# Decoder step, one core: the first two units of seven stages side by side, sums in front of the last tile, cache loads one by one, key stores last, eight banks for the first embedding

## Chip, core and metric

The kernel runs as one program on one core of a Trainium2 chip. The time is the device time of one execution in microseconds (us); it was 1290.23 as the median of three executions before the change. Beside them one execution was profiled, and all times of single instructions come from that one.

## What is computed

One inference step of a two-layer decoder trunk for 256 prompt positions and 8 sample rows together, so 264 columns. The first layer has a Mamba-2 mixer, the second an attention over a shared key/value pair; both have a half feed-forward block before and after the mixer and a gated embedding at the end:

```python
def trunk(x, p, ...):
    for i in range(DEPTH):                       # 2 layers
        x = x + 0.5 * swiglu(rmsnorm(x, w['ffn1_norm'][i]), w['ffn1_wi'][i], w['ffn1_wo'][i])
        h = rmsnorm(x, w['mix_norm'][i])
        if i < N_A_LAYERS:
            out, ... = mamba2_mixer(h, ...)
        else:
            q = rope(rmsnorm((h @ w['w_q'][j]).reshape(...), w['q_norm'][j]), pos)
            out = window_attention(q, k_all, v_all, hist_valid, w['attn_sinks'][j]) @ w['w_o'][j]
        x = x + out
        x = x + 0.5 * swiglu(rmsnorm(x, w['ffn2_norm'][i]), w['ffn2_wi'][i], w['ffn2_wo'][i])
        gate = jax.nn.sigmoid(rmsnorm(x, w['ple_norm'][i]) @ w['ple_gate'][i])
        x = x + gate * (p[i] @ w['ple_proj'][i])
        if i == N_A_LAYERS - 1:
            k_new, v_new = shared_kv(x, w['kv_norm'], w['w_kv'], w['k_norm'], pos)
```

Here `swiglu` is `(silu(gate) * up) @ wo`, and `rmsnorm` divides each row by the root of its mean square. All data are float32.

## The kernel before, in words

**Units and stages.** The weights are a list of 369 units of 128 x 1024 numbers (512 KB each), used in order by 17 stages. In the order of the program: f1i0 (first feed-forward block, inner product, 44 units), f1o0 (outer, 22), sin (mixer's input, 49), sout (16), f2i0 (44), pp0 (first embedding, 2), f2o0 (22), pg0 (gate, 8), f1i1 (44), kv (4), f1o1 (22), q (8), pp1 (2), o (8), f2i1 (44), f2o1 (22), pg1 (8). A ring of four slots takes them: SyncE loads a unit into `raw` as soon as the slot's last low half is done, ScalarE rounds it to `whi` (`round_unit`, L943), VectorE subtracts to get the low half `wlo` (`low_unit`, L1334). Both are called through `ahead(stage, i, j)`, which converts the unit four places further on than unit j of the stage, once TensorE is done with that slot.

**Products.** A product of a 128x128 weight tile and a 128x264 activation tile is three matmuls (`split_products`, L428 to L430: high by high, high by low, low by high). A unit of an inner stage ("A": f1i, sin, pg, kv, q) has 8 tiles along the depth, so 24 matmuls into one bank. A unit of an outer stage adds into all eight banks.

**A handoff.** At the end of an outer stage VectorE adds each of the eight banks to `x` (L1364), ScalarE rounds the tile to `xh` (L978) and squares it (L981), VectorE makes `xl` (L1353), and GpSimd adds the squares up (L1933, `add_squares`; in f2i0 TensorE does this with 16 passes). The next stage's first unit waits tile by tile for `xl` (`x_wait`); after its second unit TensorE sums the squares over the rows (`sums`, L460), ScalarE takes the root (`root`, L999), VectorE the reciprocal (`row_factor`, L1375), and only then can VectorE take a finished unit out of its bank (`take`, L1381). The last two units of the stage before are converted early, so that units 0 and 1 of a new stage are ready at the handoff; units 2 and 3 are converted right after the split of `x`, and units 4 and 5 (`ahead(stage, 0, 0)` and `(0, 1)`) before the root. A function of ScalarE whose table isn't loaded puts an ACT_TABLE_LOAD ahead of it.

**What orders the rest.** Each engine runs its own list in the order in which the code stands; semaphores tie them together. In f1i1 the stage kv's activations (8 `xh`, 8 `xl`) are made after the first four units. In kv, VectorE takes four units of keys and values (`kf`, `vf`), between them `ahead("kv", 0, j)`; ScalarE then takes two roots (L1223, L1224) for the key norm. GpSimd updates the state of the sample rows beside stages f2i0 to f1i1 with loads and stores of 1 MB, then issues the two cache loads `kc` and `vc` (L2082, L2083), and in q, behind the rotated keys, four stores of keys and values (L2092 to L2095), the cosine products of the queries (`query_cos`, L2102) and the small inverse roots. Loads from SyncE run in queue q1, those of GpSimd in q0. In q TensorE alternates query units, rotations (`turn`), scores (L531 to L535), transposes (L546) and weighted sums for eight pairs of heads.

```python
def first_units(stage, n, b_wait, **ops):
    for j in range(n):
        unit_a(stage, 0, j, b_wait if j < 4 else None, x_wait=(j == 0), **ops)
        if j == 1:
            sums(stage, b_wait)
```

## Time and profile before

| | |
|---|---|
| median of 3 executions | 1290.23 us (1288.71 to 1290.67) |
| the profiled execution | 1291.22 us, span 1289.4 us |
| TensorE matmuls | busy 1228.4 us, 95% |
| VectorE / ScalarE / GpSimd | 887.5 us (69%) / 690.4 us (54%) / 234.8 us (18%) |
| granted TensorE clock, mean | 0.98 |
| chain that ended last | TensorE 69%, VectorE 15%, ScalarE 7%, issue 7% |
| read from memory, mean rate | 226.87 MB, 186 GB/s |

TensorE's busy time counts matmuls that overlap, so 95% doesn't mean that 5% is all there is to gain: a matmul of 264 columns is shown with 0.28 us, while the next begins 0.12 us after it. To see what a stretch costs, one looks at the starts.

### The profile page before, as it was taken

The numbers are of one execution on the slowest core, as the hardware profiler recorded it, in microseconds if no ns is written. First come the engines' busy times: TensorE is split into PE (matmuls) and PEld (weight loads), VectorE is DVE, ScalarE is ACT, GpSimd is POOL, SyncE is SP. The second block draws the span as 40 slices with busy tenths as digits, with TensorE's granted clock in tenths as the row PEclk, the third lists the DMA queues.
The fourth block names the chain that finished last, engine by engine and source line by source line (L and its number), as shares of the span: only waits on it lengthen the run. The fifth ranks groups of instructions, "written<-read, shape, count | busy, mean of one in ns | idle before, by whom it ended". The sixth has DMA issues, their size and how long they took to land.

```text
span 1289.4 us, 26817 instructions
## 1 busy us (share of the span) xinstructions
PE 1228.4 (95%) x9921; PEld 1187.0 (92%) x9921; DVE 887.5 (69%) x1412; ACT 690.4 (54%) x1100; POOL 234.8 (18%) x333
## 2 busy tenths in 40 slices
PE   5999999789999999999999899998998999999998
PEld 5999999778898899999999799998987899999998
DVE  5677646788888876677646878786466758667447
ACT  5444436576566555555546664554364546454335
POOL 3000003112231100122344223332015201000001
PEclk8999999899999999999999899998998999999999
DMA  8555555534344445767776656756541135455552
GB/s 311 190 179 184 180 179 174 202 110 177 135 149 143 153 147 190 310 211 254 261 289 204 225 195 230 255 199 241 179 170 64 50 120 175 179 179 179 179 179 83
DMA packets 61280, 239.08 MB, mean 185 GB/s; under 512 B 7064, under 2 KB 8256, under 8 KB 56704
## 3 DMA queue, kind: packets, MB, share of 16 engines
q1 hardware_dynamic: 54864, 197.01, 43.5%
q0 software_dynamic: 6064, 40.66, 8.8%
q8 instruction: 42, 0.69, 0.2%
q10 hardware_dynamic: 288, 0.54, 0.1%
q14 instruction: 22, 0.18, 0.0%
HBM read 226.87 MB, written 13.39 MB: 186 GB/s over the span
## 4 chain that ended last, share of the span: by engine, by line
PE 69%; DVE 15%; ACT 7%; issue 7%; DMA 1%; POOL 1%; DVEq 0%; SPq 0%; ACTq 0%; POOLq 0%
PE bank L428 21%; PE bank L429 21%; PE bank L430 21%; DVE wlo L1334 3%; ACT whi L943 3%; DVE xl L1353 2%; DVE gu L1393 1%; DVE xact L1575 1%; DVE x L1364 1%; DVE gu L1381 1%; PE bank L546 1%; POOL sq L1933 1%; DMA raw<-weights 1%; PE bank L740 1%; PE bank L735 1%
## 5 line engine op out<-in xcount | busy, mean ns | idle before, releaser
L1334 DVE TENSOR_TENSOR wlo<-raw,whi 128x1024 fp32r<-128x1024 f32 x369 | 459.4, 1248 | 278.5 <-ACT whi L943 277.5
L428 PE MATMUL bank<-xh,whi 128*128 128x264 f32 x2024 | 589.1, 291 | 21.3 <-DVE xl L1353 18.4
L429 PE MATMUL bank<-xl,whi 128*128 128x264 f32 x2024 | 578.6, 286 | 0.0
L430 PE MATMUL bank<-xh,wlo 128*128 128x264 f32 x2024 | 577.9, 286 | 0.0
L943 ACT ACTIVATE whi<-raw 128x1024 fp32r<-128x1024 f32 x369 | 387.6, 1054 | 291.0 <-PE bank L430 277.5
L428 PEld LDWEIGHTS bank<-xh,whi 128*128 128x128 f32 x2024 | 386.8, 191 | 32.6 <-DVE xl L1353 15.9
L429 PEld LDWEIGHTS bank<-xl,whi 128*128 128x128 f32 x2024 | 387.0, 191 | 0.9
L430 PEld LDWEIGHTS bank<-xh,wlo 128*128 128x128 f32 x2024 | 384.7, 190 | 0.0
L428 PE MATMUL bank<-hh,whi 128*128 (+1 forms) x896 | 257.0, 287 | 5.2 <-DVE xact L1381 3.4
L430 PE MATMUL bank<-hh,wlo 128*128 (+1 forms) x896 | 256.1, 286 | 0.0
L429 PE MATMUL bank<-hl,whi 128*128 (+1 forms) x896 | 255.5, 285 | 0.0
L428 PEld LDWEIGHTS bank<-hh,whi 128*128 128x128 f32 x896 | 169.7, 189 | 7.0 <-DVE xact L1381 3.6
L429 PEld LDWEIGHTS bank<-hl,whi 128*128 128x128 f32 x896 | 170.2, 190 | 0.1
L430 PEld LDWEIGHTS bank<-hh,wlo 128*128 128x128 f32 x896 | 169.7, 189 | 0.0
L1933 POOL TENSOR_TENSOR sq<-sq 128x264 f32<-128x264 f32 x49 | 44.0, 897 | 507.6 <-ACT sq L981 502.3
L1009 ACT ACTIVATE hh<-gu 128x264 fp32r<-128x264 f32 (+1 forms) x88 | 37.3, 424 | 161.8 <-DVE gu L1393 161.8
L1381 DVE TENSOR_TENSOR gu<-bank,rstd 128x264 f32<-128x264 f32 x192 | 82.2, 430 | 19.8 <-PE bank L430 17.6
L1398 DVE TENSOR_TENSOR hl<-gu,hh 128x264 f32 (+1 forms) x88 | 42.4, 482 | 28.9 <-ACT hh L1009 28.9
L2056 POOL TENSOR_TENSOR xact<-xact,da_bc 128x512 f32<-128x512 f32 x32 | 39.5, 1235 | 106.7 <-PE bank L430 106.6
L1575 DVE SCALAR_TENSOR_TENSOR xact<-under,vs,xact 128x256 f32<-128x256 f32 x96 | 46.6, 486 | 2.3
L1393 DVE TENSOR_TENSOR gu<-gu 128x264 f32<-128x264 f32 x88 | 44.9, 511 | 0.6 <-ACT gu L1004 0.6
L1353 DVE SCALAR_TENSOR_TENSOR xl<-x,vs,xh 128x264 fp32r<-128x264 f32 x64 | 38.7, 616 | 3.1 <-ACT xh L978 3.0
(309 smaller groups left out, 1005.6 us busy)
## 6 DMA issues: line engine op xcount, KB each, us to landing
raw<-weights SPq DMA_DIRECT2D x369, 512.0 KB, 3.5
under<-ssm POOLq DMA_DIRECT2D x8, 1024.0 KB, 5.8
xact<-ssm POOLq DMA_DIRECT2D x8, 1024.0 KB, 7.0
out_ssm_s<-xact POOLq DMA_DIRECT2D x8, 1024.0 KB, 5.4
xact<-dtx_rows POOLq DMA_DIRECT2D x5, 1024.0 KB, 9.5
zs<-dtx_rows POOLq DMA_DIRECT2D x2, 1024.0 KB, 13.5
x<-xT SPq DMA_DIRECT2D x1, 1056.0 KB, 5.6
xact<-stat_rows POOLq DMA_DIRECT2D x2, 528.0 KB, 6.9
```

The source lines that it names most:

```text
L428: pe.matmul(out, whi[:, w, c], rh, start=start, stop=False)
L429: pe.matmul(out, whi[:, w, c], rl, start=False, stop=False)
L430: return pe.matmul(out, wlo[:, w, c], rh, start=False, stop=stop)
L943: act.activation(whi[:, s, :], raw[:, s, :], ACT.Copy).then_inc(hi_ready, 1)
L1334: dve.tensor_tensor(wlo[:, s, :], raw[:, s, :], whi[:, s, :].bitcast(F32), ALU.subtract).then_inc(lo_ready, 1)
L1353: dve.scalar_tensor_tensor(out=xl[:, m, :], in0=x[:, m, :], scalar=vs[:, gain + m:gain + m + 1], in1=xh[:, m, :].bitcast(F32), op0=ALU.mul ...
L1381: dve.tensor_tensor(dst, src[:, 0:N], rstd[:, :], ALU.mult).then_inc(a_free, 1)
L1393: dve.tensor_tensor(gu[:, 2 * p + 1, :], gu[:, 2 * p, :], gu[:, 2 * p + 1, :], ALU.mult).then_inc(h_ready, 1)
L1398: dve.tensor_tensor(one(hl), gu[:, 2 * p + 1, :], one(hh).bitcast(F32), ALU.subtract).then_inc(hl_ready, 1)
L1575: dve.scalar_tensor_tensor(out=out, in0=xr[:, k:k + T], scalar=vs[:, V_CW + CT * k + c:V_CW + CT * k + c + 1], in1=out, op0=ALU.mult, op1= ...
L1933: pool.tensor_tensor(sq3[:, 0, :], sq3[:, 0, :], sq3[:, m, :], ALU.add).then_inc(sq_pair, 1)
L2056: pool.tensor_tensor(by_head(part), by_head(part), da_bc[:, 2 * k:2 * k + 2, 4 * q:4 * q + 4].unsqueeze(3).to_broadcast([P, 2, 4, 64]), AL ...
```

## The change

- Seven stages (sin, f2i0, pg0, f1i1, q, f2i1, pg1) run their first two units side by side, tile by tile into two banks (`unit_pair`); `sums` stand in front of the last tile (in f1i1 behind unit 2). f1i0 is as it was.
- The table of the square root is loaded at the head of `split_x` and, in the first `gates`, at the eighth tile. The root and the reciprocal come before the conversion of units 4 and 5, which now stands behind the first takes (in sin, behind the first take).
- In q the third query unit is cut in two halves around the two rotations; the constants, the embedding's `ph` and `pl` and two conversions are moved behind the first rotations.
- GpSimd issues the second cache load once the first has landed and the keys are multiplied by the cosine. The key and value stores stand behind the last small inverse root. The memset of `minus_half` is moved to the front.
- The first embedding (pp0) writes its eight tiles into eight banks, where it used four in turn; f2o0 waits for the copies of the four upper ones.

Cut to its core (lines are shifted to the left):

```diff
+FIRST_EMBED_BANK = [4, 5, 6, 7] + [(A0["pp0"] + _m) % 4 for _m in range(4)]
...
-def first_units(stage, n, b_wait, **ops):
-    for j in range(n):
-        unit_a(stage, 0, j, b_wait if j < 4 else None, x_wait=(j == 0), **ops)
-        if j == 1:
+def unit_pair(stage, b_wait, sums_inside=True, rh=xh, rl=xl):
+    u = U0[stage]
+    banks_ = [(A0[stage] + j) % 4 for j in range(2)] if stage not in ("sin", "q") else [0, 1]
+    for j in range(2):
+        pe.wait_ge(a_free, A0[stage] + j + 1)
+        if b_wait is not None:
+            pe.wait_ge(b_free, 8 * b_wait + banks_[j] + 1)
+    pe.wait_ge(lo_ready, u + 2)
+    for k in range(KT):
+        if sums_inside and k == KT - 1:
             sums(stage, b_wait)
+        pe.wait_ge(xl_ready, XREADY[stage] + k + 1)
+        for j in range(2):
+            mm = split_products(bank[banks_[j]][:, 0:N], (u + j) % RING, k, rh[:, k, :], rl[:, k, :], k == 0, k == KT - 1)
+    mm.then_inc(unit_used, 2)
+def first_units(stage, b_wait, rh=xh, rl=xl):
+    if stage == "f1i0":
+        for j in range(4):
+            unit_a(stage, 0, j, x_wait=(j == 0))
+            if j == 1:
+                sums(stage)
+        return
+    unit_pair(stage, b_wait, stage != "f1i1", rh, rl)
+    for j in (2, 3):
+        unit_a(stage, 0, j, b_wait, rh=rh, rl=rl)
+        if j == 2 and stage == "f1i1":
+            sums(stage)
 def first_units_p(stage, b_wait):
-    for j in range(KT):
-        unit_a(stage, 0, j, x_wait=(j == 0))
-        if j == 1:
-            sums(stage, b_wait)
-def query_unit(t):
+    unit_pair(stage, b_wait)
+    for j in range(2, KT):
+        unit_a(stage, 0, j)
+def query_unit(t, tiles=range(KT)):
...
     else:
         pe.wait_ge(a_free, A0["q"] + t + 3)
-    for k in range(KT):
-        if t == 0:
-            pe.wait_ge(xl_ready, XREADY["q"] + k + 1)
+    for k in tiles:
         mm = split_products(bank[QUERY_BANK[t]][:, 0:N], u % RING, k, xh[:, k, :], xl[:, k, :], k == 0, k == KT - 1)
-    mm.then_inc(unit_used, 1)
+    if KT - 1 in tiles:
+        mm.then_inc(unit_used, 1)
...
 def ffn_in(stage, b_wait, aside=None, **ops):
-    first_units(stage, 4, b_wait, **ops)
+    first_units(stage, b_wait, **ops)
...
     for m in order:
+        if first and stage == "f2o0" and m >= 4:
+            pe.wait_ge(a_free, A0["pp0"] + m - 4 + 1 + 4)
...
         for m in range(4):
-            a = A0[stage] + 4 * j + m
-            pe.wait_ge(a_free, a + 1)
+            if j == 0:
+                if m == 1:
+                    pe.wait_ge(dtx_row, 1)
+                pe.wait_ge(a_free, A0[stage] + 1)
+            else:
+                pe.wait_ge(a_free, A0[stage] + m + 1)
             for k in range(2):
-                mm = split_products(bank[a % 4][:, 0:N], s, 2 * m + k, ph[:, k, :], pl[:, k, :], k == 0, k == 1)
+                mm = split_products(bank[FIRST_EMBED_BANK[4 * j + m]][:, 0:N], s, 2 * m + k, ph[:, k, :], pl[:, k, :], k == 0, k == 1)
...
     else:
...
     for k in range(KT):
-        if j == 0:
-            pe.wait_ge(xl_ready, XREADY["sin"] + k + 1)
...
     mm.then_inc(unit_used, 1)
-    if j == 1:
-        sums("sin", 0)
...
 for s_ in range(len(SIN)):
-    sin_unit(s_)
+    if s_ == 1:
+        unit_pair("sin", 0)
+    elif s_ > 1:
+        sin_unit(s_)
...
-query_unit(0)
-query_unit(1)
-sums("q", 3)
+unit_pair("q", 3)
 key_turn()
-query_unit(2)
+query_unit(2, range(4))
...
 turn(1)
+query_unit(2, range(4, KT))
...
 def split_x(gain, b_stage, stage=None, n=0):
+    act.preload_act_table(ACT.Sqrt)
...
-    ahead(stage, 0, 0)
-    ahead(stage, 0, 1)
-    if stage in NORM:
+    if stage == "f1i0":
+        ahead(stage, 0, 0)
+        ahead(stage, 0, 1)
         root(stage)
-    act.preload_act_table(ACT.Silu)
+        act.preload_act_table(ACT.Silu)
+    else:
+        root(stage)
+        act.preload_act_table(ACT.Silu)
+        ahead(stage, 0, 0)
+        ahead(stage, 0, 1)
...
 def gates(gate, layer, gain):
     root(gate)
+    act.preload_act_table(ACT.Sigmoid)
...
             act.activation(gu[:, j % 4, :], gu[:, j % 4, :], ACT.Sigmoid).then_inc(sig_done, 1)
+        if j == KT - 1 and gain is not None:
+            act.preload_act_table(ACT.Sqrt)
...
+root("sin")
 ahead("sin", 0, 0)
-root("sin")
...
-act.activation(ident_r, ident, ACT.Copy)
-act.activation(mask_all, mask, ACT.Copy).then_inc(mask_ready, 1)
-split_p(1)
...
-ahead("q", 0, 0)
-act.preload_act_table(ACT.Sqrt)
-ahead("q", 0, 1)
...
 query_square(0)
+query_square(1)
...
 act.activation(vtok, bank[5][:, :].rearrange("p (c n) -> p c n", c=2), ACT.Copy).then_inc(v_tok, 1)
-query_square(1)
+act.activation(ident_r, ident, ACT.Copy)
+act.activation(mask_all, mask, ACT.Copy).then_inc(mask_ready, 1)
+ahead("q", 0, 0)
 query_square(2)
+ahead("q", 0, 1)
+split_p(1)
...
-    ahead(stage, 0, 0)
-    ahead(stage, 0, 1)
-    if stage in NORM:
-        row_factor(stage)
+    if stage == "f1i0":
+        ahead(stage, 0, 0)
+        ahead(stage, 0, 1)
+    row_factor(stage)
...
     up(0, 0)
+    if stage != "f1i0":
+        ahead(stage, 0, 0)
+        ahead(stage, 0, 1)
...
             else:
                 dve.wait_ge(unit_used, U0[stage] + j + 1 + RING)
-            dve.tensor_copy(pj[layer][4 * j + m], bank[(A0[stage] + 4 * j + m) % 4][:, 0:N]).then_inc(a_free, 1)
+            dve.tensor_copy(pj[layer][4 * j + m], bank[FIRST_EMBED_BANK[4 * j + m]][:, 0:N]).then_inc(a_free, 1)
...
     if kind == "dt":
-        ahead("sin", 0, 0)
...
         dt_take()
+        ahead("sin", 0, 0)
...
                   vs[:, V_SINK:V_SINK + AH].rearrange("p (t b) -> p t b", t=PAIRS).unsqueeze(2).to_broadcast([P, PAIRS, 2, 2]), -1.0, None, ALU.mult)
-low_p(1)
-ahead("q", 0, 0)
-ahead("q", 0, 1)
...
 key_rope()
-take(qf[:, 2, :], "q", 2)
 for t in range(2):
...
     rope_add(t)
+take(qf[:, 2, :], "q", 2)
+ahead("q", 0, 0)
+ahead("q", 0, 1)
+low_p(1)
...
 pool.dma_start(kc, kcT).then_inc(cache_in, 16)
-pool.dma_start(vc, vc_in).then_inc(cache_in, 16)
+link(pool, pool_step, steps, pool.memset(minus_half, -0.5))
...
 for j in range(2):
...
     pool.tensor_tensor(gu[:, j, :], kf[:, j, :], cosT, ALU.mult).then_inc(k_cos, 1)
+pool.wait_ge(cache_in, 16)
+pool.dma_start(vc, vc_in).then_inc(cache_in, 16)
 add_squares("q")
-pool.wait_ge(k_roped, 2)
-pool.wait_ge(v_tok, 1)
-pool.dma_start(kv_p[0], kf[:, :, 128:256]).then_inc(kv_out, 16)
-pool.dma_start(kv_p[1], vf[:, :, 128:256]).then_inc(kv_out, 16)
-pool.dma_start(kv_new[0], kf[:, :, T:N]).then_inc(kv_out, 16)
-pool.dma_start(kv_new[1], vf[:, :, T:N]).then_inc(kv_out, 16)
...
-link(pool, pool_step, steps, pool.memset(minus_half, -0.5))
+pool.wait_ge(q_gains, 1)
+pool.wait_ge(k_roped, 1)
 query_cos(0)
-pool.wait_ge(q_gains, 1)
+pool.wait_ge(k_roped, 2)
...
 inverse_root(row_r, row_m, row_u, 1, dec_r)
+pool.dma_start(kv_p[0], kf[:, :, 128:256]).then_inc(kv_out, 16)
+pool.dma_start(kv_p[1], vf[:, :, 128:256]).then_inc(kv_out, 16)
+pool.dma_start(kv_new[0], kf[:, :, T:N]).then_inc(kv_out, 16)
+pool.dma_start(kv_new[1], vf[:, :, T:N]).then_inc(kv_out, 16)
```

Three places show how the order of instructions changes. TensorE at the handoff to f2i1, before, from the last tile of unit 1 (bank 2) on; `sq,cs` is the sum of squares:

```order
L428 MATMUL bank2<-xh,whi 128x264
L429 MATMUL bank2<-xl,whi 128x264
L430 MATMUL bank2<-xh,wlo 128x264
L460 MATMUL bank45<-sq,cs 128x264
L428 MATMUL bank3<-xh,whi 128x264
L429 MATMUL bank3<-xl,whi 128x264
L430 MATMUL bank3<-xh,wlo 128x264
```

and after:

```order
L433 MATMUL bank2<-xl,whi 128x264
L434 MATMUL bank2<-xh,wlo 128x264
L464 MATMUL bank45<-sq,cs 128x264
L432 MATMUL bank1<-xh,whi 128x264
L433 MATMUL bank1<-xl,whi 128x264
L434 MATMUL bank1<-xh,wlo 128x264
L432 MATMUL bank2<-xh,whi 128x264
L433 MATMUL bank2<-xl,whi 128x264
L434 MATMUL bank2<-xh,wlo 128x264
L432 MATMUL bank3<-xh,whi 128x264
L433 MATMUL bank3<-xl,whi 128x264
L434 MATMUL bank3<-xh,wlo 128x264
```

The last two tiles of both units (banks 1 and 2) now alternate, and the sum stands one tile before their end, with unit 2 (bank 3) behind.

ScalarE at the same handoff, before, from the last tile of the split on, where the four `whi` are units 2 to 5:

```order
L978 ACTIVATE xh<-x,vs 128x264
L981 ACTIVATE sq<-x 128x264
L943 ACTIVATE whi<-raw 128x1024 x4
L999 ACT_TABLE_LOAD
L999 ACTIVATE rstd<-bank,cs 128x264
L1015 ACT_TABLE_LOAD
L1004 ACTIVATE gu<-gu 128x264
L943 ACTIVATE whi<-raw 128x1024
```

and after:

```order
L1009 ACTIVATE xh<-x,vs 128x264
L1012 ACTIVATE sq<-x 128x264
L974 ACTIVATE whi<-raw 128x1024 x2
L1031 ACTIVATE rstd<-bank,cs 128x264
L1050 ACT_TABLE_LOAD
L974 ACTIVATE whi<-raw 128x1024 x2
L1036 ACTIVATE gu<-gu 128x264
L974 ACTIVATE whi<-raw 128x1024
```

One table load is gone from the front of the root (it stands before the first `xh`), and two of the four conversions stand behind the root.

GpSimd behind the last state store, up to the first cosine of the queries, before:

```order
L2082 DMA xact<-kcT 128x2048
L2083 DMA xact<-vcT 128x2048
L2084 TENSOR_SCALAR xact<-cs,vs 128x264
L2085 TENSOR_SCALAR xact<-cs,vs 128x128
L2088 TENSOR_TENSOR gu<-xact,cs 128x264 x2
L1933 TENSOR_TENSOR sq<-sq 128x264 x7
L2092 DMA out_kv_p<-xact 256x1x128
L2093 DMA out_kv_p<-xact 256x1x128
L2094 DMA out_kv_new<-xact 256x1x8
L2095 DMA out_kv_new<-xact 256x1x8
L2112 MEMSET small 128x4
L2102 TENSOR_TENSOR gu<-xact 128x264 x2
```

and after:

```order
L2123 DMA xact<-kcT 128x2048
L2124 MEMSET small 128x4
L2125 TENSOR_SCALAR xact<-cs,vs 128x264
L2126 TENSOR_SCALAR xact<-cs,vs 128x128
L2129 TENSOR_TENSOR gu<-xact,cs 128x264 x2
L2131 DMA xact<-vcT 128x2048
L1974 TENSOR_TENSOR sq<-sq 128x264 x7
L2138 TENSOR_TENSOR gu<-xact 128x264 x2
```

The load of `vcT` has moved behind the two key products, and the four stores no longer stand ahead of the cosines.

## Rows read from the trace of the kernel before

**Rows 1.** Waits of TensorE: engine, line, releaser: us in total, times, longest.

```profile
PE bank L428 <- DVE xl L1353: 18.4, 19, 8.5
```

**Rows 2.** Timeline at the handoff to f2i1: start, us, engine, line, operation, [idle before].

```profile
1062.13 0.52 ACT L978 ACTIVATE xh<-x,vs 128x264 fp32r<-128x264 f32 x1 [1.64 <-DVE x L1364]
...
1064.67 5.27 POOL L1933 TENSOR_TENSOR sq<-sq 128x264 f32<-128x264 f32 x6
...
1067.81 1.53 DVE L1353 SCALAR_TENSOR_TENSOR xl<-x,vs,xh 128x264 fp32r<-128x264 f32 x2
...
1069.73 3.57 DVE L1334 TENSOR_TENSOR wlo<-raw,whi 128x1024 fp32r<-128x1024 f32 x3 [0.39 <-ACT whi L943]
...
1072.78 0.61 PE L460 MATMUL bank<-sq,cs 128*128 128x264 f32 x2
...
1074.11 1.28 ACT L999 ACT_TABLE_LOAD   x1
...
1075.92 1.80 DVE L1375 RECIPROCAL rstd<-rstd 128x264 f32<-128x264 f32 x1 [0.57 <-ACT rstd L999]
```

**Rows 3.** Timeline of the stage sin.

```profile
219.88 1.80 DVE L1375 RECIPROCAL rstd<-rstd 128x264 f32<-128x264 f32 x1 [0.61 <-ACT rstd L999]
...
240.61 0.36 PE L809 MATMUL bank<-cs,small 64*128 64x64 f32 x1 [6.77 <-ACT small L1154]
```

**Rows 4.** Timeline at the handoff to f2i0.

```profile
504.44 3.72 PE L460 MATMUL bank<-sq,cs 128*128 128x264 f32 x16
```

**Rows 5.** Timeline of the first embedding.

```profile
634.93 0.36 PE L428 MATMUL bank<-ph,whi 128*128 128x264 f32 x1 [1.90 <-DVE xact L1446]
```

**Rows 6.** Timeline of pg0 and f1i1; one stretch: us, busy, PEclk, DMA share, GB/s.

```profile
715.93 1.07 ACT L943 ACTIVATE whi<-raw 128x1024 fp32r<-128x1024 f32 x1 [0.42 <-DMA raw<-weights]
...
718.05 1.22 DVE L1334 TENSOR_TENSOR wlo<-raw,whi 128x1024 fp32r<-128x1024 f32 x1
...
736.47 1.29 DVE L1353 SCALAR_TENSOR_TENSOR xl<-x,vs,xh 128x264 fp32r<-128x264 f32 x3
...
738.00:742.00 4.00, 4.00 (x20) 4.00 (x19) 1.23 (x1) 1.06 (x1) 0.37 (x1) 0.50 0.01 4
...
743.90 0.61 PE L460 MATMUL bank<-sq,cs 128*128 128x264 f32 x2
...
762.16 0.38 PE L428 MATMUL bank<-xh,whi 128*128 128x264 f32 x1 [0.25 <-DVE wlo L1334]
```

**Rows 7.** Timeline from kv to f1o1; DMA queues from 879 to 880 us.

```profile
872.48 0.54 POOL L2082 DMA_DIRECT2D xact<-kcT  x1 [6.07 <-DMA out_ssm_s<-xact]
...
882.96 1.06 ACT L943 ACTIVATE whi<-raw 128x1024 fp32r<-128x1024 f32 x1 [4.37 <-DMA raw<-weights]
...
885.86 1.06 ACT L943 ACTIVATE whi<-raw 128x1024 fp32r<-128x1024 f32 x1 [1.85 <-DMA raw<-weights]
...
889.14 0.59 PE L428 MATMUL bank<-hh,whi 128*128 128x264 f32 x1 [1.18 <-ACT gu L1224]
...
q0 software_dynamic: 33, 0.27, 65.6%
q1 hardware_dynamic: 33, 0.14, 32.8%
```

**Rows 8.** Timeline of the stage q.

```profile
951.97 6.20 POOL L1933 TENSOR_TENSOR sq<-sq 128x264 f32<-128x264 f32 x7 [56.16 <-ACT sq L981]
...
968.90 0.74 POOL L2092 DMA_DIRECT2D out_kv_p<-xact  x1 [10.72 <-DVE xact L1492]
...
973.80 1.01 PE L531 MATMUL bank<-hl 128*128 128x384 f32 x2 [2.23 <-DVE xact L1508]
...
982.59 1.60 PE L546 MATMUL bank<-under 128*128 128x128 f32 x12
```

**Rows 9.** Timeline of the last two units of pg1.

```profile
1282.27 0.43 DVE L1381 TENSOR_TENSOR gu<-bank,rstd 128x264 f32<-128x264 f32 x1 [1.43 <-PE bank L430]
...
1285.17 0.43 DVE L1381 TENSOR_TENSOR gu<-bank,rstd 128x264 f32<-128x264 f32 x1 [1.66 <-PE bank L430]
```

## Prediction

> **What bounds the kernel now.** I read three views in this order: what TensorE waits for, the timeline around every handoff from one stage to the next, and the DMA queues where a weight unit comes late. Inside the stages TensorE is the bound: at the end of the program VectorE takes finished units at 1282.27 and 1285.17 and had to wait for TensorE before each [rows 9]. That is 2.90 us for a unit, and with 24 matmuls in a unit 0.121 us for one matmul. Time is therefore only to be had where TensorE waits or runs slow, and nearly all of that sits at handoffs: its longest total is for the low half `xl` of the new activations, 19 waits and 18.4 us, of which 8.5 are the start of the program [rows 1]. At the others the first unit of a stage is fed one tile of `xl` at a time while the second unit, whose weights are ready, stands behind it.
>
> **The sum, place by place.** The stage f2i1 is the pattern. `xl` tiles 6 and 7 take 1.53 us for both and the last is ready at 1069.34; GpSimd has added the squares at 1069.94; the sums start at 1072.78, after two whole units [rows 2]. Side by side, six matmuls (0.73 us) go with each tile, less than the 0.77 us in which a tile comes, so that after the last tile only the sums and six matmuls are left. The sums stand in front of the last tile and wait for GpSimd, so they start at about 1070.0, the pair is through 0.73 us plus the sums later, and unit 2 starts 1072.78 - (1070.0 + 0.73) = 2.05 us earlier. Its low half is the first of three from 1069.73, ready at 1070.95, so it doesn't wait. Is the gain kept? The row factor now comes before the low halves of units 4 and 5: two conversions end at 1072.15, the reciprocal (1.80) then runs to 1074.0 where it ended at 1077.72 [rows 2], two takes bring 1074.8 and the low half of unit 4 is ready near 1076.0. TensorE wants it at 1070.98 + 2 x 2.90 = 1076.8. It is kept with 0.8 us to spare: **f2i1 2.05 us**. The last stage, pg1, has the same tiles, and its end hangs on TensorE alone [rows 9]; its sums wait for GpSimd equally, so **pg1 2.0 us**.
>
> The square root's table load leaves the path there: it stood at 1074.11 for 1.28 us [rows 2] between the sums and the root, and now runs at the head of the split, where ScalarE waits 1.64 us for the first sum `x` [rows 2]. It costs nothing as long as that wait is over 1.28 us. There the row goes against a rule. The Trainium skill (ScalarE: Activation LUTs, What ACT_TABLE_LOAD costs) gives 2.66 us for a switch, a drain of 1.38 us counted in. By that price each of the six loads moved into a split would hold the first tile 1.02 us and the total gain would be 6 us smaller; the trace shows no such drain, so I leave it out.
>
> Stage sin: the first two conversions of this stage would end 1.1 us before the third, so the reciprocal that began at 219.88 [rows 3] can begin at about 218.15, 1.73 us earlier. Behind it comes a chain of small steps on VectorE and ScalarE that ends in TensorE's wait of 6.77 us up to 240.61 [rows 3]. TensorE's own gain of some 2 us there only lengthens that wait; what counts is the chain's shift. The conversion moved behind the first take lies in VectorE's wait for the exponential. **sin 1.7 us**, from 0 (if the three state loads, now issued some 3 us earlier, hold a weight unit) to 2.
>
> Stage f2i0 adds its squares on TensorE: 16 passes, 3.3 of the 3.72 us [rows 4], and these stay. Only the gaps between tiles go: **0.8 us** (0.5 to 1.1).
>
> The first embedding waits 1.90 us at 634.93 for a bank that VectorE has yet to copy [rows 5]. With eight banks the wait goes, but the next stage wants four of them back, and the same copies are then late. Between 0 and 1.9: **1.0 us**.
>
> Stages pg0 and f1i1 belong together, since in pg0 VectorE's chain of take, gate, add, conversion and `xl` decides. The row factor is 1.8 us earlier, as in sin, but the chain meets a weight unit that landed at 715.93 [rows 6] behind two GpSimd loads, which don't move: ScalarE's half of the conversion ends at 717.0 and VectorE's begins at 718.05 [rows 6], so 1.05 us of the 1.8 are left. The last `xl` of f1i1 is ready at 737.76 now [rows 6], 736.7 then. TensorE runs at the granted clock 0.50 there, its 1.2 GHz level, with 20 matmuls in 4 us, and the sums come at 743.90 [rows 6]. With the pair, 6 matmuls are left after the last tile where 27 were. If the clock stays low until about 741.5, the sums, which stand behind unit 2 here, come near 743.5, hardly earlier than now; the root is then 1.3 us earlier by its table load and 1.2 by the conversion it no longer waits for. But now two conversions (2.44 us) stand behind it, before unit 8, whose low half TensorE waited for at 762.16 [rows 6] after VectorE's eight `xl` of the key stage. By my count it is ready at about 760.5: **1.6 us** for both stages, from 0 to 4.8 (if the clock stays at its 2.4 GHz level throughout).
>
> The largest place is the key stage and the start of f1o1. A cache load of 1 MB is issued at 872.48 and a second right behind it, and weight units issued right behind land so late that ScalarE can convert them only from 882.96 (4.37 us of waiting) and from 885.86 [rows 7]. The key values' last take and their square roots stand behind these two conversions on VectorE and ScalarE; TensorE waits for them until 889.14 [rows 7]. While both run, queue 0 moves 0.27 MB/us and queue 1, the weights', 0.14, with 33 packets each [rows 7]. With one cache load instead of two, 1 MB at 0.27 MB/us from about 874.5 ends near 878.5; the weights then have the whole rate, and their two units land at about 879 and 881. Then conversion, table load (1.28), two roots (about 1.0) give 884.3 in place of 889.1: 4.8 us. And the 18 matmuls that ran behind that wait on the low clock need 0.1 us less each if it isn't there for the clock to fall in: 1.8 us, of which I take 1.5. **6.3 us**, from 2.9 (weights land at 881 and 883) to 7.4. The second cache load goes out behind the key norms, beside f1o1, where a unit has some 8 us to land. The Trainium skill (DMA: Bandwidth & Descriptors, Queues, rings and completion order) says that each DMA engine takes packets of its queues in turn; the equal packets of the row agree. By it one cache load still takes two thirds of the bytes while it lasts, which is the low end above.
>
> In the stage q the four key stores are issued from 968.90 on, GpSimd's first two `q` cosines come behind them, and TensorE's first scores wait for what follows until 973.80 [rows 8]. The stores go behind the last query. The new order, worked out from durations: sums at 958.2, when GpSimd's squares end (951.97 + 6.20 [rows 8]), root 958.9, reciprocal (behind two conversions) 960.6 to 962.4, takes 963.2, key rotation 964.8, first cosine 964.4 to 965.2, second rotation 966.2, half a unit of filler to 967.7, scores at 967.7. Then VectorE has a take, two conversions and the low half of `p` (4.1 us) before the first maxima, at 971.5; exponentials 975.2, first transposes 976.6 in place of 982.59 [rows 8]. From there on the rhythm is TensorE's and doesn't change: **q 6.0 us**, from 4.5 (GpSimd slower beside VectorE) to 7.
>
> Sum: 2.05 + 2.0 + 1.7 + 0.8 + 1.0 + 1.6 + 6.3 + 6.0 = 21.45 us. The profiled execution took 1291.22 us for a span of 1289.4; it is 1.0 over the median 1290.23. 1291.22 - 21.45 = 1269.8, and against the median **1268.8 us**.
>
> **Rivals.** (A) One cache load holds the weights as long as two did, because the share and not the volume decides: the key stage gives 0, and the time is 1275.1. For it: the first unit behind the loads could only be converted 10.5 us after them. Against it: the 1 MB store just before, for which the loads waited 6.07 us [rows 7], held no conversion up. (B) The clock of f1i1 stays up, since twice the work comes with each tile: 3.2 us more, 1265.6. Against it: even then three quarters of the time is waiting. (C) VectorE gives back what TensorE gains, because conversions moved behind the row factor end later than TensorE wants them: sin, pg0 and f1i1 at 0, f2i1 at 1.0; 1273.1. The margin of 0.8 us in f2i1 decides. (D) The other side: pairs are fed thinly enough that TensorE's clock falls at all seven handoffs. A spell as in f1i1 (20 matmuls in 4 us where 33 would go) costs 3.9 us over its 8 us, seven are 27.3: 1268.8 + 27.3 = 1296.1, slower. It decides if TensorE waits as long between a pair's tiles as it does in f1i1; at six of seven places the rows leave 0.6 us at most for a tile.
>
> **How the numbers follow.** Forecast 0.60, A 0.12, B 0.10, C 0.12, D 0.03, anything else 0.03. The range from 1263 to 1277.5 takes in A, B and C and leaves out D and joint mishaps. A measurement tells about 0.2% (2.6 us) from no change: faster by more 0.95, within 0.02, slower 0.03.
>
> **What would show it.** In the profile after: sums of f2i1 within 0.2 us of GpSimd's last square; no table load between sums and root; conversions of the two weight units at 879 to 881 instead of 883 to 886, and a granted clock of 1.0 through f1o1's first unit; first scores about 6 us nearer to the last `xl` of q; the wait before `small` in sin as long as now. The forecast is wrong if weight units still land after 9 us beside one cache load, or if VectorE's conversion of unit 4 becomes what TensorE waits for in the feed-forward stages.

## The result and the profile after

The median of five executions is 1277.60 us (1276.56 to 1282.18), against 1290.23 before: the ratio is 0.9917 (0.9895 to 0.9939). In a second group of runs the same kernel took 1275.25 us beside 1289.52 (ratio 0.9876, 0.9859 to 0.9893). So by the medians the kernel is 12.6 to 14.3 us faster where 21.4 were forecast, and the median lies 0.1 us outside the range. The times are scattered more widely than before: three of the eleven executions took 1281.5 to 1282.5 us, the other eight 1272.8 to 1277.8. The profiled one took 1281.47 for a span of 1279.4, so it is one of the three.

To see where the gain is, I cut both profiled executions at points that each has: the first sum `x<-bank,x` of each handoff and the sums of the key squares.

| stretch | before, us | after, us | gain | forecast |
|---|---|---|---|---|
| start, to the first sum in front of sin | 207.61 | 208.16 | -0.55 | 0 |
| sin and sout | 286.76 | 283.97 | 2.79 | 1.7 |
| f2i0, pp0, f2o0 | 204.64 | 202.75 | 1.89 | 0.8 + 1.0 |
| pg0, f1i1, kv up to the key sums | 181.44 | 181.82 | -0.38 | 1.6 |
| from there over f1o1 to q | 69.43 | 68.35 | 1.08 | 6.3 |
| q, pp1, o | 111.79 | 110.37 | 1.42 | 6.0 |
| f2i1, f2o1 | 194.32 | 192.43 | 1.89 | 2.05 |
| pg1 | 33.40 | 31.60 | 1.80 | 2.0 |

Four terms came about as forecast. One was too small (sin), and three failed: pg0 with f1i1, the key stage, q. In the waits of TensorE (engine, line, releaser: us in total, times, longest) the answer to [rows 1] is that 18.4 us over 19 waits for `xl` have become 11.7 over 4. The waits for `wlo`, the low halves, have grown from 0.9 us over 3 to 7.1 over 6. A wait for the exponentials is new:

```profile
PE bank L432 <- DVE xl L1391: 11.7, 4, 8.5
PE bank L432 <- DVE wlo L1372: 7.1, 6, 2.5
...
PE bank L558 <- ACT small L1295: 2.4, 1, 2.4
```

The handoff to f2i1, the answer to [rows 2] (timeline: start, us, engine, line, operation, [idle before]):

```profile
1057.52 6.22 POOL L1974 TENSOR_TENSOR sq<-sq 128x264 f32<-128x264 f32 x7 [35.60 <-ACT sq L1012]
...
1061.57 1.55 DVE L1391 SCALAR_TENSOR_TENSOR xl<-x,vs,xh 128x264 fp32r<-128x264 f32 x2
...
1063.87 0.63 PE L464 MATMUL bank<-sq,cs 128*128 128x264 f32 x2
...
1065.04 1.28 ACT L1050 ACT_TABLE_LOAD   x1
...
1065.88 1.79 DVE L1413 RECIPROCAL rstd<-rstd 128x264 f32<-128x264 f32 x1
```

GpSimd's squares (`sq<-sq`) end at 1063.74 and the sums start 0.13 us later, as forecast. No table load stands between sums and root; the one that is left runs behind the root. The reciprocal starts 2.0 us behind the sums, where it was 3.1.

pg0 and f1i1, the answer to [rows 6]:

```profile
713.38 1.06 ACT L974 ACTIVATE whi<-raw 128x1024 fp32r<-128x1024 f32 x1 [3.87 <-DMA raw<-weights]
...
724.63 0.56 PE L432 MATMUL bank<-xh,whi 128*128 128x264 f32 x1 [2.52 <-DVE wlo L1372]
...
733.46 0.96 POOL L1974 TENSOR_TENSOR sq<-sq 128x264 f32<-128x264 f32 x1 [0.34 <-ACT sq L1012]
...
740.19 0.61 PE L464 MATMUL bank<-sq,cs 128*128 128x264 f32 x2
...
746.03 0.39 PE L432 MATMUL bank<-xh,whi 128*128 128x264 f32 x1 [2.34 <-DVE wlo L1372]
```

ScalarE waits 3.87 us for the weight unit for which it waited 0.42 before. The last `xl` of f1i1 is ready at 734.71: the program was 4.1 us ahead of before at the start of pg0, and here it is 3.05 ahead. The longest wait for a low half (2.52 us) stands at the head of the pair in f1i1, which starts only when the low halves of both its units are there; behind it TensorE waits for `xl` twice more. The sums come 5.8 us after the last square (at 734.42), because unit 2 stands ahead of them, and TensorE is at the 1.2 GHz level for the first part of that time (granted clock 0.57 from 734 to 738 us, 1.00 from 738 to 741). Then it waits 2.34 us for the low half of unit 4, which was moved behind the row factor. From the last `xl` to the key sums the program gains 0.7 us.

The key stage, the answer to [rows 7]; the last row is a stretch of four us (from, to, length, busy times and counts of PE, PEld, DVE, ACT, POOL, then the granted clock, DMA share, GB/s):

```profile
868.61 0.54 POOL L2123 DMA_DIRECT2D xact<-kcT  x1 [5.95 <-DMA out_ssm_s<-xact]
...
879.49 2.09 ACT L974 ACTIVATE whi<-raw 128x1024 fp32r<-128x1024 f32 x2 [4.66 <-DMA raw<-weights]
...
882.20 0.59 PE L432 MATMUL bank<-hh,whi 128*128 128x264 f32 x1 [3.73 <-DVE xact L1419]
...
884.00:888.00 4.00, 4.00 (x21) 4.00 (x21) 3.96 (x3) 1.06 (x1) 0.15 (x1) 0.52 0.58 189
```

The whole program is 3.76 us ahead of before at the key sums. The first conversion is 3.47 us ahead and so a little late by comparison; the second follows at once and has gained 1.5 us. The wait of TensorE (3.73 us) is still there, and so is the spell at the 1.2 GHz level behind it (granted clock 0.52 in the last row). The two weight units behind the cache load took 10.1 and 9.3 us to land.

In q, the answer to [rows 8], the first scores come 17.80 us after the first sum of the stage, where it was 23.92:

```profile
962.85 0.51 PE L558 MATMUL bank<-hl 128*128 128x384 f32 x2
...
970.62 0.98 PE L558 MATMUL bank<-hl 128*128 128x384 f32 x2 [2.42 <-ACT small L1295]
...
973.12 2.29 PE L573 MATMUL bank<-under 128*128 128x128 f32 x9
...
980.91 0.61 PE L558 MATMUL bank<-hl 128*128 128x384 f32 x2
```

That is 6.1 us, the forecast. Yet the third scores (980.91) come only 3.0 us earlier than before by the same count: 10.3 us pass between second and third, where before it was 7.6. The first transposes (973.12) are 4.6 us earlier, where the sum had 6.0. The second scores take 0.98 us for their first two matmuls, the third 0.61.

### The profile page after: what moved, and what is told of

It is laid out like the page before. It is cut to its first block, busy times and chain, and to the rows that moved or that the text cites. A ratio compares the mean times of both kernels' runs of the same rounds, so it can differ in the third digit from the quotient of the medians.

```text
span 1279.4 us, 26823 instructions
## 1 busy us (share of the span) xinstructions
PE 1224.1 (96%) x9921; PEld 1187.4 (93%) x9921; DVE 885.9 (69%) x1412; ACT 691.6 (54%) x1101; POOL 234.0 (18%) x333
## 4 chain that ended last, share of the span: by engine, by line
PE 71%; DVE 14%; issue 6%; ACT 6%; DMA 2%; POOL 1%; DVEq 0%; SPq 0%; ACTq 0%; POOLq 0%
PE bank L432 21%; PE bank L433 21%; PE bank L434 21%; DVE wlo L1372 4%; ACT whi L974 2%; DMA raw<-weights 1%; DVE xact L1616 1%; DVE gu L1431 1%; DVE xl L1391 1%; DVE gu L1419 1%; PE bank L573 1%; POOL sq L1974 1%; DVE x L1402 1%; PE bank L773 1%; PE bank L768 1%
## 5 line engine op out<-in xcount | busy, mean ns | idle before, releaser
L432 PE MATMUL bank<-xh,whi 128*128 128x264 f32 x2024 | 586.4, 290 | 20.4 <-DVE xl L1391 11.7
## 6 DMA issues: line engine op xcount, KB each, us to landing
xact<-dtx_rows POOLq DMA_DIRECT2D x5, 1024.0 KB, 10.6
```

What stands on the lines that cost most here:

```text
L432: pe.matmul(out, whi[:, w, c], rh, start=start, stop=False)
```

## The experiments

The first four kernels are the changed one with one edit or none. The others are built on the second of them, with both cache loads late, so that again one place at a time differs. The table has what the profiled executions gave; the column "low" is the time at the 1.2 GHz level in two stretches of q to o (12 to 38 and 60 to 90 us after the first sum), worked out as twice the part by which the mean granted clock of a stretch is under 1, times its length. The column "median" has all executions of a kernel, the others the profiled one alone. In three columns the same code repeats within 0.1 us (f2i1 with f2o1, pg1, and f2i0 to f2o0, which isn't shown), but not in all: pg0 to the key sums took 180.5 to 182.2 us in the eight profiles whose code is the same there.

| kernel | pg0, f1i1 | key, f1o1 | q, pp1, o | low | f2i1, f2o1 | pg1 | median |
|---|---|---|---|---|---|---|---|
| before | 181.4 | 69.4 | 111.8 | 14.0 | 194.3 | 33.4 | 1290.23 |
| after | 181.8 | 68.3 | 110.4 | 13.4 | 192.4 | 31.6 | 1277.60 |
| after, again | 182.2 | 67.9 | 110.5 | 13.4 | 192.4 | 31.6 | 1275.25 |
| both cache loads late | 181.9 | 62.4 | 111.9 | 16.8 | 192.4 | 31.6 | 1276.39 |
| cache loads together | 180.5 | 67.4 | 109.2 | 9.8 | 192.4 | 31.6 | 1279.36 |
| key stores early | 182.2 | 63.9 | 111.5 | 16.6 | 192.4 | 31.6 | 1277.37 |
| maxima first | 181.6 | 62.8 | 106.9 | 10.4 | 192.4 | 31.6 | 1272.03 |
| f1i1, unit 4 first | 182.1 | 62.4 | 111.9 | 16.8 | 192.4 | 31.6 | 1274.59 |
| pg0, load later | 180.8 | 62.4 | 105.9 | 3.6 | 192.4 | 31.6 | 1270.12 |
| no pairs at the end | 181.8 | 62.3 | 107.3 | 7.0 | 194.3 | 33.4 | 1279.82 |
| f1i1, sums inside | 178.1 | 62.3 | 108.8 | 10.2 | 192.4 | 31.6 | 1271.00 |
| four edits together | 176.6 | 62.4 | 104.5 | 3.6 | 192.4 | 31.6 | 1264.48 |
| filler matmuls | 182.1 | 62.4 | 108.9 | 10.0 | 192.4 | 31.6 | 1272.34 |

**The changed kernel again**

> The changed kernel as it is, beside the others of this group, as their measure. Its profiled execution (1281.47 us) stood some 4 us over three of its other four. Theory one: the 4 us come from one place, where a transfer of GpSimd meets the weight loads (stage pg0 or the key stage); then one of the two execution times shows weight units landing later there, and the two groups of times appear again, near 1277 and 1282. Theory two: they come from chance in the granted clock; then the spells at the 1.2 GHz level differ in number between the executions and the landings don't. The time expected is 1276.5 to 1282.

Six executions: 1272.81, 1273.10, 1274.90, 1275.60, 1277.80 and, the profiled one, 1282.49. Its profile agrees with the first one (110.5 for 110.4 in q, 67.9 for 68.3 in the key stage). The two groups of times appeared again. Both profiles lie in the upper group, so they show what the kernel does in three executions of eleven, and the others gain more. No profile shows where, so neither theory is decided; the next runs show two places where the same code takes different times, the key stage and q.

**Both cache loads behind the key norms**

```diff
-            pool.dma_start(kc, kcT).then_inc(cache_in, 16)
...
                 pool.tensor_tensor(gu[:, j, :], kf[:, j, :], cosT, ALU.mult).then_inc(k_cos, 1)
+            pool.dma_start(kc, kcT).then_inc(cache_in, 16)
             pool.wait_ge(cache_in, 16)
             pool.dma_start(vc, vc_in).then_inc(cache_in, 16)
```

> The first cache load too is issued behind the key norms, the second still when the first has landed; no cache load lies beside the key stage any more. Theory V (the one load left beside the weights is what still holds them): the two conversions of weight units that ended their wait at 879.5 and 880.5 in the changed kernel come at about 875 and 876.5, TensorE's wait of 4.0 us and the clock spell behind it go, and the kernel is 4 to 6 us faster than the changed one. Theory S (the weights are late there for another reason, the store of the last state or SyncE's queue): the two conversions stay within 1 us of where they are, and the time is the same within 1 us. If the load meets another stage's weights instead, f1o1 shows it as a DMA wait of ScalarE behind 890 us.

The conversions and what follows, and the load at its new place:

```profile
876.35 1.06 ACT L974 ACTIVATE whi<-raw 128x1024 fp32r<-128x1024 f32 x1 [1.18 <-PE bank L434]
...
879.61 3.45 DVE L1521 RECIPROCAL gu<-gu 128x528 f32<-128x528 f32 x1 [0.94 <-ACT gu L1264]
...
886.25 0.60 POOL L2129 DMA_DIRECT2D xact<-kcT  x1
```

ScalarE no longer waits for a transfer but for TensorE, the reciprocal of the key norm is at 879.61 where it was 883.78, and the stretch from the key sums to q takes 62.4 us in place of 68.3. It was 62.3 to 62.8 in all eight kernels built this way. For the stage theory V holds: the one load that the change left beside the weights was still the cause. Its 4 to 6 us less for the whole kernel didn't come: the median gained nothing against the changed kernel (1276.39 and 1275.25), while the slowest execution is 1276.61 and not 1282.49. q took 111.9 us here, 1.5 more than after, with 16.8 us at the low level.

**Both cache loads together again**

```diff
             pool.dma_start(kc, kcT).then_inc(cache_in, 16)
+            pool.dma_start(vc, vc_in).then_inc(cache_in, 16)
...
-            pool.wait_ge(cache_in, 16)
-            pool.dma_start(vc, vc_in).then_inc(cache_in, 16)
```

> Both cache loads are issued one behind the other again, as before the change; all else as changed. By the forecast's step (the volume of the second load holds the weights) this gives back 3 to 6 us. By rival A (one load holds the weights as long as two) it gives back 0 to 1 us. The comparison of the two profiles showed the key stage and f1o1 only 1.1 us shorter after the change, so I expect 1 us: 0.5 to 2.

The two ways of reading disagree. The median is 4.1 us over that of the changed kernel on the same chip (1279.36 and 1275.25, ratios 0.9914 and 0.9876), as the volume would have it. The key stretch of the profiles is no longer: 67.4 us for 67.9. The profiles of the changed kernel are both of its upper group. In the kernel of the next paragraph, which is the changed one up to q, the stretch took 63.9. There the two weight units are converted from 878.49 on, 0.7 us behind the key sums (2.8 in the changed kernel), TensorE waits 1.62 us in place of 3.73, and its granted clock is 1.00 from 880 to 888 us. So one load beside the weights costs between 1.5 and 6.0 us against none (62.4), depending on the execution. What the second load costs isn't shown: the stretch says nothing, one pair of medians 4 us, and the first group of the changed kernel has the same ratio to before (0.9917) as this one (0.9914).

**Key stores early again**

```diff
             add_squares("q")
+            pool.wait_ge(k_roped, 2)
+            pool.wait_ge(v_tok, 1)
+            pool.dma_start(kv_p[0], kf[:, :, 128:256]).then_inc(kv_out, 16)
...
```

> The four stores of keys and values stand in front of the queries' cosines again; all else as changed. If GpSimd's issue of the stores (2.4 us from the first to the end of the last in the profile of before) was what held the first scores, they come 2.4 to 3.3 us later than in the changed kernel, counted from the first x of the stage. If the time follows the first scores, the kernel is slower by as much. If the clock spell and the exponentials decide the start of the attention instead, most of it is swallowed: slower by 0 to 1 us.

VectorE waits for GpSimd behind the stores:

```profile
958.90 2.02 POOL L2144 TENSOR_TENSOR gu<-xact 128x264 f32<-128x264 f32 x2
...
960.26 0.96 DVE L1549 TENSOR_TENSOR xact<-gu 128x264 f32<-128x264 f32 x1 [3.38 <-POOL gu L2144]
```

The cosines start 17.25 us after the first sum of q (14.41 in the changed kernel), VectorE's rotation 18.61 (15.33), the first scores 19.89 (17.80). The first two are late by the stores. For the first scores this isn't shown: in the next kernel the stores are late, its rotation starts at 15.35, and its first scores come at 19.90 all the same, because TensorE is at the 1.2 GHz level ahead of them for as long as here. Stretches from 14.4 us after the first sum on, here and in the next kernel, the granted clock being the third number from the end:

```profile
956.00:960.00 4.00, 3.09 (x13) 2.80 (x13) 0.77 (x3) 1.28 (x2) 3.44 (x6) 0.62 0.25 71
954.00:958.00 4.00, 3.10 (x12) 2.92 (x13) 2.41 (x7) 1.16 (x2) 3.45 (x7) 0.61 0.03 11
```

The whole of q took 1.0 to 1.1 us more with the stores early, and 3.2 us more at the low level account for 1.4 of that at the rate found below. So nothing of the stores is seen at the end of the stage.

**First maxima before the low half of unit 5 and of p**

```diff
             ahead("q", 0, 0)
-            ahead("q", 0, 1)
-            low_p(1)
             for s_ in range(3, PAIRS):
                 maxima(s_ - 3)
+                if s_ == 3:
+                    ahead("q", 0, 1)
+                if s_ == 4:
+                    low_p(1)
```

> As the kernel with both cache loads behind the key norms, and in the stage q VectorE takes the first maxima before the low half of unit 5, and the low half of p after the second maxima. Before this, the first maxima began 4.0 us after the first scores (2.6 before the change), and the first exponentials, for which TensorE waits 2.4 us before its second scores, 1.4 after them. Theory one (VectorE's order holds the exponentials, the wait makes the clock fall): first maxima at 2.2 to 2.6 us after the first scores, second scores 1.4 to 1.9 us earlier, and the spell at the 1.2 GHz level behind them shorter; the stage q is 1.5 to 3.5 us shorter. Theory two (the clock spell comes from the waits ahead of the first scores and stays): the second scores are earlier, but the third are only 0 to 1 us earlier.

First scores at 959.41 (19.90 us after the first sum), first maxima at 961.89 (2.5 us later, 4.0 before this edit), second scores at 965.67: 6.3 us after the first, where it was 7.8. q took 106.9 us against 111.9, and even against the 109.2 us of the kernel with about the same time at the low level (9.8 and 10.4) it is 2.3 less; the 5.0 us are more than the 3.5 expected, and the difference goes with the low clock. Theory one holds: VectorE's order held the exponentials.

**f1i1: unit 4 before the row factor**

```diff
+                elif stage == "f1i1":
+                    ahead(stage, 0, 0)
+                    root(stage)
...
+                if stage == "f1i1":
+                    ahead(stage, 0, 0)
                 row_factor(stage)
```

> As the kernel with both cache loads behind the key norms, and in the stage f1i1 alone unit 4 is converted before the root and the row factor again, unit 5 behind the first takes. In the changed kernel TensorE waited 2.5 us for the low half of unit 4 there. If that wait (rival C) is what gives the gain back, the stretch from the last xl of f1i1 to the key sums is 1.5 to 2.6 us shorter. If VectorE is late there anyway (for the eight xl of the key stage), the wait only moves to another low half and the stretch stays within 0.5 us.

The wait for unit 4 is gone and one for unit 8 has taken its place:

```profile
758.11 0.44 PE L432 MATMUL bank<-xh,whi 128*128 128x264 f32 x1 [1.82 <-DVE wlo L1377]
```

It was 0.53 us at that unit in the changed kernel, and the stretch takes 182.1 us, as with both loads late (181.9). VectorE is late as a whole in f1i1, and the order of its work does not mend that. The forecast's rival C names the right engine, but the old order of the conversion is no remedy.

**pg0: second load after four units**

```diff
                 if q == 5:
-                    pool.wait_ge(unit_used, U0["pg0"] + RING)
+                    pool.wait_ge(unit_used, U0["pg0"] + 4 + RING)
```

> As the kernel with both cache loads behind the key norms, and in pg0 GpSimd's second load of 1 MB (dtx rows) is issued after four units of the stage, not at once behind the first. In the changed kernel ScalarE waited 3.9 us for a weight unit that landed behind both loads, and the stretch from the first gated x to the last xl of f1i1 was 2.0 to 3.3 us longer than before the change. If the second load holds the unit, it lands 2 to 3.5 us earlier and the stretch is 1.5 to 3 us shorter. If one load of 1 MB holds it as long, within 0.5 us. If the load only meets the next units, they show the wait instead and the stretch stays the same.

```profile
710.53 1.06 ACT L974 ACTIVATE whi<-raw 128x1024 fp32r<-128x1024 f32 x1 [0.62 <-DMA raw<-weights]
...
711.19 0.55 POOL L2086 DMA_DIRECT2D under<-dtx_rows  x1 [7.12 <-PE bank L434]
```

The wait for the weight unit is 0.62 us instead of 3.9. The stretch from the first gated `x` to the last `xl` of f1i1 shrank by 2.2 us (25.3 to 23.1), and TensorE's wait at the head of the pair from 2.6 to 0.4. Up to the key sums only 1.1 are left (180.8), which is within what kernels with the old place of the load took (180.5 to 182.2). With the sums moved as well, the load is worth 1.5 us (178.1 with the sums moved, 176.6 in the kernel with all four edits). This execution has another thing to show. Its q is the same code as in the changed kernel, and here TensorE stayed at its 2.4 GHz level. Stretches of this kernel, then of the one with both loads late, around the second scores:

```profile
959.00:963.00 4.00, 2.62 (x21) 2.21 (x19) 3.90 (x9) 2.08 (x6) 2.43 (x5) 1.00 0.78 242
963.00:967.00 4.00, 2.96 (x24) 2.58 (x25) 3.26 (x10) 2.15 (x7) 2.21 (x5) 1.00 0.40 152
```

```profile
963.00:967.00 4.00, 1.69 (x7) 1.04 (x8) 3.30 (x9) 3.43 (x11) 1.21 (x3) 0.72 0.63 211
967.00:971.00 4.00, 4.00 (x22) 3.69 (x19) 2.02 (x7) 1.47 (x7) 1.51 (x5) 0.50 0.09 35
```

With the clock at 1.00 here, and 3.6 us at the low level later on, q took 105.9 us, 5.9 less than before the change: the forecast 6.0. The trace of before has 14.0 us at the low level itself, but they cost little behind the first scores: from the second scores to the end of the stage it took 80.6 us and this kernel 80.3. With 16.8 us at the low level the same instructions took 111.9. Between them lie 107.3 (7.0 us low, the next kernel) and 110.4 (13.4, the changed kernel). That is 0.45 us for each us at the low level. What decides how long the clock stays low isn't shown.

**No pairs in f2i1 and pg1**

```diff
+                if stage == "f2i1":
+                    for j in range(4):
+                        unit_a(stage, 0, j, b_wait, x_wait=(j == 0), rh=rh, rl=rl)
+                        if j == 1:
+                            sums(stage, b_wait)
+                    return
...
```

> As the kernel with both cache loads behind the key norms, but in f2i1 and pg1 the first two units run one after the other again with the sums behind the second; table load, root and row factor stay as changed. If the pair itself gives the gain of the two stages (1.9 us each), both are 1.8 to 2.1 us longer, 3.6 to 4.2 together. If part of it comes from the table load and the order of root and conversions, they are longer by less: 0.5 to 1.5 each.

Both stages are back at 194.3 and 33.4 us, to the last 0.03 us. The whole gain of the two is the pair's (with the sums in it); an earlier table load and another order of root and conversions are worth nothing there while TensorE is the limit. The median is 3.4 us over that of the kernel with both cache loads late, near the 3.6 to 4.2 expected; the profiled execution (1275.46) is the fastest of its four.

**f1i1: sums in front of the last tile**

```diff
-                unit_pair(stage, b_wait, stage != "f1i1", rh, rl)
+                unit_pair(stage, b_wait, True, rh, rl)
...
-                    if j == 2 and stage == "f1i1":
-                        sums(stage)
```

> As the kernel with both cache loads behind the key norms, and in f1i1 too the sums stand in front of the pair's last tile, not behind unit 2. So far unit 2 stood before them at the 1.2 GHz level, and they came 5.5 us after GpSimd's last square. Expected: sums within 1 us of that square, the reciprocal 4 to 5 us earlier, and the conversions of units 4 and 5 no longer waited for (2.6 us). If TensorE's clock is the limit there, part of it stays: the stretch from the last xl to the key sums is 2 to 3 us shorter. If VectorE's later work (eight xl of the key stage, unit 8) is the limit, it is 0 to 1 us shorter.

```profile
732.88 0.96 POOL L1972 TENSOR_TENSOR sq<-sq 128x264 f32<-128x264 f32 x1 [0.34 <-ACT sq L1010]
...
735.70 0.82 PE L464 MATMUL bank<-sq,cs 128*128 128x264 f32 x2
...
737.07 1.80 DVE L1411 RECIPROCAL rstd<-rstd 128x264 f32<-128x264 f32 x1 [2.93 <-ACT rstd L1029]
```

The sums are 1.9 us behind the last square (5.8 so far), the reciprocal 3.6 us earlier than with both loads late (740.63), and the stretch is 3.8 us shorter. Sums and reciprocal gained less than expected and the stretch more; the wait for unit 4 is gone. So it was the place of the sums that made VectorE late.

**The four edits together**

Both loads late, maxima first, the load of pg0 later, sums inside in f1i1.

> All the edits that the runs pointed to, together: both cache loads behind the key norms, first maxima before the low half of unit 5, second load of pg0 after four units, sums of f1i1 in front of the pair's last tile. Against the kernel before, counted by stages: sin 2.6, f2i0 and pp0 1.9, pg0 and f1i1 1 to 3.5, key stage and f1o1 7.1, q 5 to 6.5, f2i1 1.9, pg1 1.8, less 0.7 at the start: 20.6 to 24 us less, 1266 to 1269.5. If the edits share one cover (the clock spells above all), the sum falls short by 2 us or more.

The five executions took 1264.12 to 1264.79 us, the ratio to before is 0.9805 (0.9791 to 0.9818). This is 25 us faster than the kernel before and 11 to 13 faster than the changed one, and nothing is left of the scatter. pg0 and f1i1 gave 4.8 us against before, q 7.3. The time is 1.5 us under the range that I expected (1266 to 1269.5), so nothing is seen of a cover that the edits share.

**Filler matmuls in front of the wait for the exponentials**

```diff
+                    if t == 1:
+                        for _ in range(20):
+                            pe.matmul(bank[7][:, 0:192], ident_r, mask_all[:, 0:192], start=True, stop=True)
                     pe.wait_ge(s_exp, t)
```

> As the kernel with both cache loads behind the key norms, and twenty matmuls of 192 columns whose result nobody reads stand on TensorE before its wait for the first exponentials (2.3 to 2.4 us, before the second scores). If the wait is what the granted clock falls after, the spell at the 1.2 GHz level behind it goes, transposes and the unit behind them run at 0.12 us a matmul, and the third scores come 1.5 to 3 us earlier after the first (18.2 us so far, 15.3 in the execution that had no spell). If the spell has its cause ahead of the first scores, it is as long as before and the third scores stay within 0.5 us. Should the fillers run past the wait, the second scores show it by coming later than 7.8 us after the first.

```profile
959.05 0.75 PE L561 MATMUL bank<-hl 128*128 128x384 f32 x2
...
964.29 2.57 PE L557 MATMUL bank<-hl 128*128 128x192 f32 x20
...
966.76 0.61 PE L561 MATMUL bank<-hl 128*128 128x384 f32 x2
...
974.29 0.62 PE L561 MATMUL bank<-hl 128*128 128x384 f32 x2
```

Second scores 7.7 us after the first, as ever, and the third 15.2, not 18.2. No low clock stood behind the wait, which is as expected if the wait is what it falls after. It is one execution, and two of the nine profiles with this order of VectorE and no filler showed no spell there either, so it supports this and doesn't prove it.

## Why the prediction was wrong, point by point

**Right.** The pairs of f2i1 and pg1: 1.89 and 1.80 us for 2.05 and 2.0, down to the sums 0.13 us behind GpSimd; without the pairs both are gone. f2i0 with the eight banks: 1.89 for 1.8. The first embedding starts 134.7 us behind the first sum of f2i0, where it was 135.6, and from there the banks give the other 1.0. TensorE's wait for a copy is now 0.93 us, at the start of f2o0, in place of 1.90: half of it came back, as the term had it. The table load in the split costs nothing: `xh` starts 0.46 us after the first sum of f2i1 in both kernels. So the price of the Trainium skill (ScalarE: Activation LUTs, What ACT_TABLE_LOAD costs), with its drain, is not seen at this place. The first scores came 6.1 us earlier.

**q, 6.0 us: the step that failed** is "From there on the rhythm is TensorE's and doesn't change". Up to the first scores the times came as worked out (what the stores have in them isn't separated). Then the first maxima came 4.0 us behind the scores, because unit 5 and `p` stood ahead of them, TensorE waited 2.42 us, and its clock stood at the 1.2 GHz level over transposes and the next unit. Both losses had their rows: I had counted 4.1 us of VectorE's work before the maxima and did not ask what TensorE does meanwhile. The sum had priced the clock in f1i1 and in the key stage, in q it had not, although the trace of before shows spells there. Measured, the term is -0.1 to 5.9 us, and 5.9 in the kernel where no spell stood behind the wait.

**The key stage, 6.3 us.** The step "1 MB at 0.27 MB/us from about 874.5 ends near 878.5; the weights then have the whole rate, and their two units land at about 879 and 881" is counted on the time of the kernel before. The conversions began at 879.49 and 880.5, which is 883.3 and 884.3 on that time, since the program was 3.8 us ahead. That conversions at 879 to 881 were named as a sign of the forecast, and came, is luck: the first had not gained on the program, which was 3.8 us ahead. The load left alone was not a faster one (issues: KB, us to landing; then the queues from 873 to 877 us: packets, MB, share):

```profile
xact<-kcT POOLq DMA_DIRECT2D x1, 1024.0 KB, 10.6
...
q1 hardware_dynamic: 265, 0.99, 68.1%
q0 software_dynamic: 63, 0.43, 25.5%
```

It took 10.6 us where I had given it 6: beside the weights queue 0 moved 0.11 MB/us in these four us, where the sum had 0.27 to the end. So only the second unit gained, 1.5 us, and the wait of TensorE and the spell behind it stayed. The term is right for the kernel with no cache load beside the stage (7.1 us), is 5.6 in one execution with one load, and 1.1 to 1.6 in both profiles of the changed kernel. Rival A ("One cache load holds the weights as long as two did") describes these two. Both things that the forecast had named as showing it wrong came about: weight units landed after 9 to 10 us beside one load, and in f1i1 TensorE waited for the conversion of unit 4.

**pg0 and f1i1, 1.6 us.** I let the landing of the weight unit stay where it was, at 715.93, while the program arrives 4.1 us earlier. It came at 713.38, only 2.6 us earlier. The GpSimd loads started 4.1 us earlier, but the unit that is issued behind them took 8.9 us where it had taken 7.3. So the last `xl` of f1i1 lost 1.1 us where the sum had it gain 1.05, and that is the whole miss. With the second load later it gained 1.05. The rest of f1i1 gave 0.7 us, about what the sum had (0.55). It could have given 3.8 more: the sums stood behind unit 2. I had seen that they came "hardly earlier than now" and gave it no price.

**sin, 1.7 us.** TensorE's wait ended 1.5 us earlier, as forecast, though the wait itself is 5.7 us and not 6.8 as I had said: of TensorE's own gain of some 2 us only 0.5 is left there, with a new wait of 1.0 us for a low half (at 224.92). Another 1.2 us arises between 246 and 305 us and was there in each of the runs (2.4 to 3.0 in all). Its cause isn't settled. The start of the program is 0.3 us shorter to 1.2 us longer than in the one profile of before, in a stage that the change does not touch; this too stays open.

Together: of what is missing (8.8 us against the first median, 11.5 between the profiles), the key stage has 5.2, q 4.6 and pg0 2.0; in the first two a wait stayed and a spell of low clock stands behind it. Rival D had the right mechanism at the wrong place: it put the low clock into all the pairs, where outside f1i1 it didn't fall, and not into the waits behind them. Its price was too high, too: 40 matmuls in 8 us where they need 4.8 at full clock cost 3.2 us and not 3.9.

## What to carry to other kernels

A gain on TensorE's path is only kept where the next wait is short: ask what the engine does while the freed chain runs, and price the low clock behind each wait that stays. Count a landing from its issue and from what lies ahead of it, not from a rate; and take the loads that nobody needs yet out of the stage altogether rather than half of them. A stretch-by-stretch table over several kernels tells chance from effect better than medians, once it is known how well each stretch repeats: some within 0.1 us, pg0 to the key sums within 1.7, q within 6.

## What was unexpected of the hardware

A weight unit that is issued behind two loads of GpSimd moves nothing for a while. In the changed kernel a unit was issued between 704 and 705 and took 8.9 us (issues: KB, us to landing). From 705 to 708 us queue 0 sent 155 packets, and queue 1, which has the weights, has no row at all. Nor has it in the kernel before from 709 to 712 us, behind a unit issued at 708.56 (the last line):

```profile
raw<-weights SPq DMA_DIRECT2D x1, 512.0 KB, 8.9
```

```profile
q0 software_dynamic: 155, 1.14, 90.8%
...
q0 software_dynamic: 152, 1.11, 91.3%
```

In both kernels the first weight packet goes out as the first of the two GpSimd loads lands (708.13 and 708.15 us; 712.32 and 712.17 before), 3.7 and 3.8 us after the issue. So this silence was in the trace of before, and it is not what made the unit later. What differs is the second GpSimd load: it landed 5.0 us behind the first, 3.6 before, and the unit 0.2 us behind it in both. Its last three packets came one by one, 0.46 us apart (711.35 to 712.28). Why it took longer is open. In [rows 7] both queues sent 33 packets in a us, which agrees with turns. The Trainium skill (DMA: Bandwidth & Descriptors, Queues, rings and completion order) has each engine take packets of its queues in turn; the three us without weight packets do not show that.

The second surprise is how much of one kernel's time goes with the clock: the same instructions of q took 105.9 to 111.9 us, with 3.6 and 16.8 us at the 1.2 GHz level. What decides between them isn't shown.
